# Streaming the columns of the moving operand and of the accumulator from the last to the first in every matmul of a weight stream

## The reference

```python
for i in range(2):
    h = rms_norm(x, mix_norm[i])
    x = x + (mamba2_mixer(h, ...) if i == 0 else nsa_mixer(h, ...))   # h @ w_in ... @ w_out
    h = rms_norm(x, ffn_norm[i])
    gate, up = split(h @ w_gu[i])                                     # 2048 -> 2 x 5632
    x = x + (silu(causal_dwconv(gate)) * up) @ w_down[i]              # 5632 -> 2048
```

## Time and profile before

| | |
|---|---|
| median of 3 runs | 2669.05 us (2667.92 to 2672.13) |
| time of the profiled execution | 2667.43 us |
| its span in the profile | 2665.7 us |
| TensorE matmuls busy | 2625.5 us, 98% of the span |
| TensorE weight loads busy | 2292.3 us, 86% |
| VectorE busy | 1788.8 us, 67% |
| ScalarE busy | 1429.2 us, 54% |
| mean granted TensorE clock | 0.996 of full speed |

### The profile page before, as it was taken

How to read it: one execution, slowest core, us unless ns; L and a number is a source line. 1 busy time by engine, 2 the same in 40 slices (tenths; PEclk the granted TensorE clock), 3 DMA queues, 4 the chain that set the end, 5 groups by cost and what they waited for, 6 DMA issues and landing times. The chain is left out here.

```text
span 2665.7 us, 46463 instructions
## 1 busy us (share of the span) xinstructions
PE 2625.5 (98%) x15411; PEld 2292.3 (86%) x15411; DVE 1788.8 (67%) x2612; ACT 1429.2 (54%) x2210; POOL 196.4 (7%) x179
## 2 busy tenths in 40 slices
PE   7999999999999999999999999999999999999999
PEld 6888888888888888888888888888888888888888
DVE  7677777765677777775555756665677777775444
ACT  5676766654455555554444545555455555554443
POOL 0111111121200000000111000001300000000000
PEclk9999999999999999999999999999999999999999
DMA  5655555556555555556666565322555555556665
GB/s 185 218 191 194 191 191 185 193 171 189 180 184 188 188 187 187 188 187 188 189 187 195 175 197 191 103 95 93 183 181 189 189 189 188 189 188 183 188 188 168
DMA packets 135254, 481.94 MB, mean 181 GB/s; under 512 B 15104, under 2 KB 17152, under 8 KB 134160
## 3 DMA queue, kind: packets, MB, share of 16 engines
q1 hardware_dynamic: 132480, 467.72, 55.6%
q0 software_dynamic: 2336, 12.65, 1.4%
q10 hardware_dynamic: 368, 0.65, 0.1%
HBM read 478.80 MB, written 2.16 MB: 180 GB/s over the span
## 5 line engine op out<-in xcount | busy, mean ns | idle before, releaser
L969 DVE TENSOR_TENSOR w_lo<-raw,w_hi 128x1024 fp32r<-128x1024 f32 x900 | 1102.1, 1225 | 720.9 <-ACT w_hi L350 719.8
L682 PE MATMUL ps<-xn,w_hi 128*128 128x512 f32 x4768 | 1509.1, 398 | 17.3 <-DVE xn L995 10.7
L350 ACT ACTIVATE w_hi<-raw 128x1024 fp32r<-128x1024 f32 x900 | 938.7, 1044 | 889.5 <-PE ps L684 870.7
L684 PEld LDWEIGHTS ps<-xn,w_lo 128*128 128x128 f32 x4768 | 896.9, 188 | 212.2
L684 PE MATMUL ps<-xn,w_lo 128*128 128x256 f32 x4768 | 938.2, 278 | 0.0
L682 PEld LDWEIGHTS ps<-xn,w_hi 128*128 128x128 f32 x4768 | 728.4, 189 | 26.0 <-DVE xn L995 11.3
L682 PE MATMUL ps<-hid,w_hi 128*128 128x512 f32 x1408 | 446.9, 395 | 0.0
L684 PEld LDWEIGHTS ps<-hid,w_lo 128*128 128x128 f32 x1408 | 264.6, 188 | 57.1
L684 PE MATMUL ps<-hid,w_lo 128*128 128x256 f32 x1408 | 288.0, 279 | 0.0
L682 PEld LDWEIGHTS ps<-hid,w_hi 128*128 128x128 f32 x1408 | 219.6, 189 | 5.5
L682 PE MATMUL ps<-y_ssm,w_hi 128*128 128x512 f32 x512 | 161.6, 397 | 0.0
(11 more groups left out here) (238 smaller groups left out, 1762.9 us busy)
## 6 DMA issues: line engine op xcount, KB each, us to landing
raw<-w_gu SPq DMA_DIRECT2D x352, 512.0 KB, 3.8
raw<-w_ssm_in SPq DMA_DIRECT2D x162, 512.0 KB, 3.6
raw<-w_down SPq DMA_DIRECT2D x128, 448.0 KB, 3.4
raw<-w_nsa_in SPq DMA_DIRECT2D x82, 512.0 KB, 3.6
raw<-w_ssm_out SPq DMA_DIRECT2D x64, 512.0 KB, 4.5
raw<-w_down SPq DMA_DIRECT2D x64, 512.0 KB, 3.6
raw<-w_nsa_out SPq DMA_DIRECT2D x32, 512.0 KB, 4.0
wcum<-cum_scratch POOLq DMA_DIRECT2D x8, 1024.0 KB, 7.3
```

What stands on the lines that cost most here:

```text
L350: act.activation(w_hi[:, slot, 0:n * P], raw[:, slot, 0:n * P], ACT.Copy).then_inc(unit_rounded, 1)
L682: pe.matmul(acc[:, 0:2 * n], w_hi[:, slot, cols], x[:, kb, 0:2 * n], start=(kb == 0), stop=False)
L684: mm = pe.matmul(acc[:, n:2 * n], w_lo[:, slot, cols], x[:, kb, 0:n], start=False, stop=(kb == p.blocks - 1))
L969: TT(w_lo[:, slot, 0:n * P], raw[:, slot, 0:n * P], w_hi[:, slot, 0:n * P].bitcast(F32), ALU.subtract).then_inc(unit_split, 1)
```

## The change

The matmul keeps its weights, its 512 (or 256) moving columns and its accumulator columns. Only the sequence changes: both the moving operand and the accumulator are given with a step of -1, so that column 511 is taken first and column 0 last (for L684: moving columns 255 down to 0, accumulator columns 511 down to 256). Each moving column still meets the same accumulator column.

```diff
                     for kb, cols in pair:
-                        pe.matmul(acc[:, 0:2 * n], w_hi[:, slot, cols], x[:, kb, 0:2 * n], start=(kb == 0), stop=False)
+                        pe.matmul(acc[:, 2 * n - 1::-1], w_hi[:, slot, cols], x[:, kb, 2 * n - 1::-1], start=(kb == 0), stop=False)
                     for kb, cols in pair:
-                        mm = pe.matmul(acc[:, n:2 * n], w_lo[:, slot, cols], x[:, kb, 0:n], start=False, stop=(kb == p.blocks - 1))
+                        mm = pe.matmul(acc[:, 2 * n - 1:n - 1:-1], w_lo[:, slot, cols], x[:, kb, n - 1::-1], start=False, stop=(kb == p.blocks - 1))
```

## The result

The changed kernel takes 2703.93 us (median of 4 runs, 2701.32 to 2706.30) against 2670.59 us of the kernel before (4 runs): ratio 1.0126, 95% interval 1.0108 to 1.0143. It is slower, by six times what a measurement of this kernel can tell from no change. I had forecast no change.

What follows compares the result with a forecast made beforehand. TensorE's matmul stream was taken to bound the kernel; columns, odd start, accumulator revisit, fixed part and weights summed to 0 us, giving a median of 2669 us, with an 8-in-10 range of 2650 to 4250 us.

Steps and rivals of the forecast that it cites:

- the fixed part: The 4.4 ns per stream matmul beyond its columns, 61 us in all: taken as unchanged, bounds -61 to +61 us.
- TensorE bounds the kernel, and nothing covers a loss: TensorE is busy 2625.5 of 2665.7 us and other engines wait for it, so the span gains any loss in full.
- It is the streaming of TensorE itself.: The matmul stream's rate, about 0.697 us per two blocks, is TensorE's own and not set by other engines' traffic.
- 0.442 ns a column and 4.4 ns a matmul: Split of L682's and L684's cost: 2357 us for columns plus 61 us for matmuls, together 2419 us, 91% of the span.
- The columns themselves: Cost per column walked downwards: neighbours stay neighbours, so zero taken; upper bounds 1520 or 3668 us more.
- The Trainium skill's rule on 16-byte lines: SBUF wants at least two hits a line; a downward fp32 walk gives four like an upward one, so 0 us.
- The odd start: First moving element now at column 511 or 255: zero, since VectorE took 482 against 480 ns with odd starts.
- The accumulator's revisit, and the write: Accumulator columns updated again in PSUM: nearest revisit stays 256 columns away in either direction, so zero.
- the Trainium skill's sentence on PSUM: If a reversed, gapless output counts as non-contiguous, the rule speaks against the change; it gives no figure.
- Rival 2: A small price at each matmul's start, from last address first or odd first element: 2675 to 2730 us, chance 0.08.
- the same for 512 and 256 columns: Profile sign of a changed price at the start: a few ns in each matmul start, equal for both widths.
- Rival 1: Downward walk served one column at a time in read or update: 4190, 5026 or 6337 us, chance 0.31.

Runs made afterwards that it cites:

- one_col: Kernel before, with every matmul of the stream reading its first moving column 512 or 256 times (step 0): 2536.25 us, ratio 0.9498.
- in_line_down: Kernel before, moving operand read in groups of four columns, groups first to last, columns inside each group descending; write forwards: ratio 1.0004.
- lines_down: Kernel before, moving operand read in groups of four columns, groups last to first, columns inside each group ascending; write forwards: ratio 1.0122.
- groups16_down: Kernel before, moving operand read in groups of 16 columns (64 bytes), groups last to first, ascending inside; write forwards: ratio 1.0123.
- odd_fwd: Kernel before, moving operand read forwards but from an odd column, one column off: 2657.47 us, ratio 0.9954.
- shift3: Kernel before, forward walks, its four activation tensors laid out 3 columns (12 bytes) further on: 2663.32 us, ratio 0.9967.
- shift1: Kernel before, forward walks, its four activation tensors laid out 1 column (4 bytes) further on: 2714.45 us, ratio 1.0164.
- write_back: Kernel before, both matmuls reading forwards but writing the accumulator backwards: 2668.90 us, ratio 0.9997.
- hi_back: Kernel before, only the 512-column matmuls of L682 walking backwards, L684 forwards: 2705.16 us, ratio 1.0134.
- lo_back: Kernel before, only the 256-column matmuls of L684 walking backwards, L682 forwards: 2681.66 us, ratio 1.0041.
- unit_back: Changed kernel's backward walks, but all of a unit's L682 and then all its L684 instead of pairs: 2691.57 us, ratio 1.0072 to the kernel before.
- even_back: Changed kernel, but the backward read starts at an even column (510 or 254), one column off: 2753.32 us, ratio 1.0308 to the kernel before.
- weights_odd_fwd: Kernel before, with the weights of each matmul read one column further on or back: 2688.77 us, ratio 1.0080.
- one_weight_fwd: Kernel before, forward walks, all 128 weight columns of each load being the same column (step 0): 2659.93 us, ratio 0.9953.
- unit_fwd: Kernel before, forward walks, but all of a unit's L682 and then all its L684 instead of pairs: 2677.99 us, ratio 1.0017.

## Why the prediction was wrong

The step that failed is the one on the fixed part, "I take zero": each of the 13,888 matmuls lost 2.4 ns on average, 33.9 us in the span. Before it the forecast took for granted that a stream so close to its clock does not feel how it is read. Step by step:

- *TensorE bounds the kernel, and nothing covers a loss.* Right: the period grew by 8 ns in `hid` and 10 in the other streams, 33 us in 3472 periods, and the span by 33.9.
- *"It is the streaming of TensorE itself."* Right about the other engines: the loss is there in full where VectorE and ScalarE stand still (0.705 us). But here the error begins. I had seen that a column takes more than one clock of 0.417 ns and passed over it in a bracket. `one_col` shows 42 ns a period that go with the walk over the columns. A stream that its read holds back already can feel how it is read. The matmuls of L780, at 216 ns, were in the trace to compare with, and so was the alternation of single intervals (236 and 231, 112 and 119 ns) between periods that do the same work.
- *0.442 ns a column and 4.4 ns a matmul.* This split borrowed the 117.6 ns of `cmp`. The stream's own starts in the kernel before, 233.15 ns after an L682 and 115.25 after an L684 on average, would give 0.46 ns a column and leave -2.65 ns for the fixed part. So the sum of a period was right, its split was not, and the bounds of 61 us on the fixed part had no measured size under them.
- *The columns themselves: "I take the lower end, zero".* The argument, that each piece is touched once and left complete, holds inside 16 bytes (`in_line_down`, 1.0004) and fails for the order of the pieces (`lines_down`, 1.0122). It fails as an argument, though the price does not show as one per column: in the two kernels with one weight column it is 2.1 ns for 512 columns and 2.2 for 256. The Trainium skill's rule on 16-byte lines (SBUF, "Door 1: The DMA port swizzle"), by which the sum was 0 us, asks for two hits on a line; `lines_down` and `groups16_down` (1.0123) have four, as the kernel before, and lose in full. The rule says nothing on the order in which lines are taken.
- *The odd start: zero.* The conclusion holds for the loss: `groups16_down` has it without an odd start. The reason, from VectorE's rows, did not carry over to TensorE: `odd_fwd`, `shift3` and `shift1` move its time by -0.5 to +1.6%.
- *The accumulator's revisit, and the write: zero.* Right, `write_back` 0.9997. So the Trainium skill's sentence on PSUM (PSUM, "Specifications (TRN2)"), that "any non-contiguous AP slows matmuls significantly", does not describe a reversed, gapless output like this one.
- *The fixed part: "I take zero".* This is the term that moved. Rival 2 had it: 33.9 us / 13,888 = 2.4 ns a matmul, and 2703.9 us lies between its 2675 and 2730. I gave it 0.08, since it had nothing in the rows for it. Of its two reasons, the odd first column is refuted by `groups16_down`. Something at the start is neither shown nor excluded, but one clock of 0.417 ns would be far too small. Its sign, "the same for 512 and 256 columns", is met in the two kernels with one weight column and not in the changed kernel, where the time after an L682 grew by 1.4 ns on average and that after an L684 by 3.5.
- *Rival 1*, with 0.31 and prices from 4190 us, priced a loss of adjacency that does not occur. It alone made the range run to 4250 us, so that the measured 2703.9 lies inside the range says little for the forecast. L1257's row, of another engine and with a step of 16, was no guide to a step of -1.

What stays open is the mechanism below this. The loss belongs to the moving read and to the order of pieces of 16 to 64 bytes. It goes by the matmul rather than by the column or the step, and little of it hangs on how the weights are read. Against a plain price per matmul stands that `hi_back` costs as much as both, `lo_back` a third, and `unit_back` half. Whether it is where a walk starts, where it ends or the jump to the next, these runs do not tell apart.

## What to carry to other kernels

Before an address pattern is called free on an engine that bounds the kernel, compare its rate with the same engine's rate where the read is light (a step of 0; another operand kind in the same trace is a first hint): a gap, here 42 of 697 ns, says that the pattern can matter. Look at single intervals and not only at their mean, since an alternation between neighbours that do the same work is a sign of address dependence. In an fp32r stream like this one leave the moving operand ascending; the order inside 16 bytes and the direction of the PSUM write were free to choose. And before a gain is read off a kernel's time alone, compare runs at the same mean clock: `shift3` shows 7 us otherwise, where its matmuls save 12.

## What the runs showed of the hardware

- An fp32r matmul's start-to-start time depends on where its moving operand begins: period 697 ns at 0 modulo 4 columns, 693 at 3 (`shift3`), 710 to 713 at 1 (`shift1`); backwards 706 to 707 from 3 and 720 to 724 from 2 (`even_back`).
- Walking the moving operand down costs 8 to 10 ns a period, also when only groups of 16 columns are taken from the last to the first (`groups16_down`, 706.7); the order inside 16 bytes (`in_line_down`, 1.0004) and the direction of the PSUM write (`write_back`, 0.9997) cost nothing.
- The start-to-start time also depends on where the weights lie: one column off costs 0.8% (`weights_odd_fwd`), and reading a single weight column 128 times gains 0.5% (`one_weight_fwd`).
- Reading one column over and over brings fp32r to 216 to 218 ns for 512 columns and 109 to 112 for 256, 5% of the kernel (`one_col`).
- Changing the order of loads and matmuls in a unit (`unit_fwd`) moves single intervals between 226 and 236 ns for the same 512 columns, with nearly the same sum (1.0017).
